# Sample attention one step deeper, new probabilities through the gate's bank, mask and decays stored once

## The chip, the cores and the metric

The kernel runs on one core of a Trainium2 chip. The metric is the device time of one execution in microseconds (us). The core has TensorE (PE, with its weight loads as PEld), VectorE (DVE), ScalarE (ACT), GpSimd (POOL), whose part here is to issue DMAs, and SyncE (SP), which issues the other DMAs. The accumulators lie in PSUM, 8 banks of 128 partitions by 512 float32.

## What is computed

It is one inference step of a two-layer encoder for 256 prompt rows and for 8 requests of 16 new rows ("samples") with 512 cached keys each. All is float32. A layer is a SwiGLU block, a token mixer and a second SwiGLU block. The mixer has three attention branches of 6 heads by 64:

```
sb:  a = sigmoid(z) * prod of sigmoid(-z) over the later keys (strictly causal)
fox: p = softmax(z + decay of the key's row and head)
dsa: p = softmax(z + mask), mask = the top 132 of 528 keys by an indexer's score
y = sum over the branches of sigmoid(gate_n) * (o_n @ w_branch_n);  out = y @ w_out
```

The change touches the samples' attention: 8 requests x 3 branches x 3 head pairs.

## The kernel before

One head pair of one request is a group. A unit is 4 groups, so that 4 groups x 2 heads x 16 queries fill 128 partitions. There are NU = 6 units for each branch and NSTEP = 18 steps in each layer, steps 0 to 5 for sb, 6 to 11 for fox and 12 to 17 for dsa. For unit s the work is:

- keys: `turn_three(s)` and `turn_fourth(s)` (L1113) transpose the cached keys of the 4 groups on PE, three into banks 0 to 2, the fourth into bank 3 or 0. ACT copies them to `KT[s % 2]` (L1611, L1612, L1617, `kt_free`).
- scores (L1187): 4 groups, banks 4 and 5. DVE adds the bias (L2328) and the mask of the new keys (L2333). For fox and dsa the bias comes from `BX[s % 2]`, loaded by POOL (L1718) from a DRAM scratch, and DVE takes the row maximum (L2341).
- ACT makes the probabilities: two sigmoids for sb (L1629, L1630) or Exp (L1632). For sb DVE then runs a reverse product scan (L2047) and a product (L2346).
- `turn_probs` (L1158) transposes the 512 old columns into bank 6, `turn_new_probs` (L1164) the 16 new ones into bank 7. DVE copies both to `PTS` (L2296, L2298).
- `values` (L1178) multiplies by the values into bank 7, `output_rows` on DVE (L2304 or L2306 and L2307) scales them into `OU`, `output` on PE (L1147) folds the rows into bank 7, and DVE copies them to `OT` (L2290).

PE's order in step s, written by hand, is: scores(s), output(s-2), turn_probs(s-1), turn_three(s+2), turn_new_probs(s-1), half a gate tile, values(s-1), turn_fourth(s+2). A gate half (L1138) is four of the eight k-slices of a tile of 384 columns in bank 3. Its sum stays open in that bank from one half to the next, and the twelve halves lie in the steps of `GATE_UNIT`. DVE's order is: scores' bias(s), output(s-2), copies of the probabilities(s-1), maximum or scan(s), rounds of the top-k, output_rows(s-1). One round (L2313, L2316) takes the 8 largest scores out of the indexer's rows. There are 17 rounds, in the steps of `ROUND_S`.

When the rounds are over, in step 9, SP stores the mask (L587): 8 DMAs write each row six times, once per head. The decays of fox are stored earlier (L539) with each row sixteen times. POOL's load for step 12 waits for the mask's store (`msk_stored`). Three buffers hold cached keys: the load of key block n (L572, SP's queue) waits until block n-3 has been transposed. Four buffers hold values (L1700, L1706, POOL's queue), and a load waits for `values` of the block four before. A block of keys or of values (one request, one branch) is 768 KB, and a step uses 4/3 of a block of either kind.

Of the kernel before, what the change touches and what calls it, by code (L numbers as in the profile page):

```python
# [20 lines left out]
P = 128  # L21
# [99 lines left out]
def unit_spans(s):  # L121

    out, i = [], 0
    while i < UNIT:
        n, a = unit_groups(s)[i]
        k = min(NPAIR - a, UNIT - i)
        out.append((i, i + k, n % NB, a))
        i += k
    return out

# [7 lines left out]
def program(nc, t):  # L138
    with ExitStack() as ctx:
# [121 lines left out]
        OU = NORM[:, (PC + 1) * P:(PC + 2) * P]  # L261
# [67 lines left out]
        ps_ready = sem("sprobs_ready")  # L329
        st_ready, st_copied = sem("st_ready"), sem("st_copied")  # L330
# [38 lines left out]
        def _(sp):  # L369
# [126 lines left out]
            for l in range(DEPTH):  # L496
# [5 lines left out]
                for i in range(N_PROJ):  # L502
# [75 lines left out]
                for s in range(-2, NSTEP):  # L578
# [5 lines left out]
                    if s == max(ROUND_S):  # L584
                        sp.wait_ge(msk_ready, l * 3 + 3)
                        for b in range(NB):
                            sp.dma_start(m_s[b * NH * NT:(b + 1) * NH * NT, :].rearrange("(h t) k -> t h k", t=NT),  # L587
                                         WKS[b * NT:(b + 1) * NT, :][:, None, :].to_broadcast([NT, NH, KEYS])).then_inc(msk_stored, 16)

                w = t["w_branch"][l].rearrange("n (k p) d -> p (n k) d", p=P)  # L590
                for i in range(N_BRANCH):
                    r = R_BRANCH + i
                    if i < 2:
                        sp.wait_ge(gate_ready, l * 24 + 21 + 3 * i)
                        sp.wait_ge(msk_stored, (l + 1) * NB * 16)
# [16 lines left out]
        def _(pe):  # L612
# [253 lines left out]
            for l in range(DEPTH):  # L866
# [248 lines left out]

                def turn_three(s):
# [6 lines left out]
                def turn_fourth(s):  # L1123

                    if s >= 2:
                        pe.wait_ge(kt_free, 3 * (l * NSTEP + s) + 2)
                    turn_group(s, 3, 3 if s < 2 else 0).then_inc(kt_ready, 1)

                def gate_half(n, half):

                    r = R_GATE + n // 3 - 1
                    if half == 0:
                        if n % 3 == 0:
                            full(l, r)
# [1298 lines left out]
```

## Time and profile before

| | |
|---|---|
| time, 3 runs | 2439.22 us median (2438.75 to 2440.55) |
| profiled execution | 2444.67 us, span 2442.9 us |
| busy over the span | PE 2366.5 (97%), PEld 2044.6, DVE 1240.9, ACT 555.7, POOL 75.3 us |
| DMA | 396.57 MB, mean 162 GB/s |
| mean granted TensorE clock | 0.992 |

The times of the table's first line are device times. The span is what the profiler recorded from the first instruction to the last, and the profiled execution took 1.8 us more than it. PE's busy share counts its pipelined matmuls, so 97% is not PE at its peak. Each layer has one sample attention, of 141 us, and both show the same pattern.

### The profile page before, as it was taken

Reading aid. Unit: us, or ns where it says so; the run is one execution under the profiler, and the core shown is the slowest. Engines: PE = TensorE matmul, PEld = TensorE weight load, DVE = VectorE, ACT = ScalarE, POOL = GpSimd, SP = SyncE. Lnnn points to the kernel's source line nnn. Section 1 sums busy time; section 2 is a strip of 40 time slices with the busy share of each in tenths; the row PEclk is TensorE's granted clock in tenths of the full one; section 3 lists DMA queues with packets and bytes.
Section 4 is the critical chain, followed back from the end, with each engine's and each line's share of the span. In section 5 each row is a group of like instructions: output and inputs, shape, how many; then the busy total and the mean of one; then the engine's idle time right before and its main releaser. Section 6 shows DMA issues by size and latency. Waiting matters only on the chain.

```text
span 2442.9 us, 41219 instructions
## 1 busy us (share of the span) xinstructions
PE 2366.5 (97%) x17088; PEld 2044.6 (84%) x17088; DVE 1240.9 (51%) x2630; ACT 555.7 (23%) x1290; POOL 75.3 (3%) x124
## 2 busy tenths in 40 slices
PE   7999999999998999999999999999999989999998
PEld 6999996886665589999989999878756656999998
DVE  3656422534665426565265663235365844366742
ACT  3000022113553322001130000211235432410011
POOL 0000000000022000000000000000000220000000
PEclk9999999999999999999999999999999999999999
DMA  8354243773389342542325533447634883323232
GB/s 322 128 186 162 95 143 122 234 251 100 117 282 338 130 152 103 181 164 93 133 104 177 185 135 108 146 145 255 203 104 169 306 295 126 105 83 125 95 117 74
DMA packets 298634, 396.57 MB, mean 162 GB/s; under 512 B 31309, under 2 KB 243145, under 8 KB 298450
## 3 DMA queue, kind: packets, MB, share of 16 engines
q1 hardware_dynamic: 278690, 339.66, 41.3%
q0 software_dynamic: 12672, 45.42, 5.3%
q10 hardware_dynamic: 7088, 8.87, 1.0%
q8 instruction: 136, 2.23, 0.4%
q14 instruction: 48, 0.39, 0.0%
HBM read 378.54 MB, written 15.37 MB: 161 GB/s over the span
## 4 chain that ended last, share of the span: by engine, by line
PE 88%; DMA 4%; DVE 3%; SPq 2%; ACT 2%; issue 1%; DVEq 0%; ACTq 0%; POOLq 0%
PE PS L681 30%; PE PS L779 12%; PE PS L986 6%; PE PS L1228 4%; PE PS L934 4%; PE PS L880 3%; PE PS L651 2%; PE PS L827 2%; PE PS L835 2%; PE PS L956 2%; PE PS L720 2%; PE PS L1113 2%; DMA BIG<-w_ada 2%; PE PS L1138 2%; PE PS L1250 2%; PE PS L1242 2%
## 5 line engine op out<-in xcount | busy, mean ns | idle before, releaser
L681 PE MATMUL PS<-OT,RING 128*128 128x192 f32 x1280 | 234.2, 326 | 0.0
L681 PE MATMUL PS<-H,RING 128*128 128x192 f32 x1280 | 223.4, 328 | 0.0
L681 PE MATMUL PS<-OT,QR 128*128 128x192 f32 x1280 | 221.1, 326 | 0.0
L681 PEld LDWEIGHTS PS<-OT,RING 128*128 128x128 f32 x1280 | 212.4, 190 | 0.0
L681 PEld LDWEIGHTS PS<-H,RING 128*128 128x128 f32 x1280 | 208.4, 190 | 4.4 <-issue 4.1
L681 PEld LDWEIGHTS PS<-OT,QR 128*128 128x128 f32 x1280 | 210.2, 190 | 0.0
L1356 ACT ACTIVATE QR<-QR 128x384 f32<-128x384 f32 x80 | 41.8, 522 | 530.9 <-DVE QR L1916 530.9
L986 PE MATMUL PS<-H,RING 128*128 128x384 f32 x480 | 160.9, 490 | 0.0
L986 PEld LDWEIGHTS PS<-H,RING 128*128 128x128 f32 x480 | 89.1, 190 | 61.5 <-issue 4.7
L681 PE MATMUL PS<-H,QR 128*128 128x192 f32 x640 | 117.1, 326 | 0.0
L681 PEld LDWEIGHTS PS<-H,QR 128*128 128x128 f32 x640 | 106.2, 190 | 0.0
L1916 DVE TENSOR_TENSOR QR<-PS,QR 128x384 f32<-128x384 f32 x80 | 44.6, 557 | 110.7 <-PE PS L681 110.7
L1228 PE MATMUL PS<-OT,RING 128*128 128x384 f32 x288 | 93.4, 487 | 0.8 <-DVE OT L2290 0.8
L880 PE MATMUL PS<-RING,H 128*128 128x384 f32 (+1 forms) x288 | 90.9, 472 | 0.0
L779 PE MATMUL PS<-BIG,RING 128*128 128x192 f32 x528 | 89.7, 326 | 0.0
L1228 PEld LDWEIGHTS PS<-OT,RING 128*128 128x128 f32 x288 | 54.6, 190 | 38.7 <-DVE OT L2290 1.0
L779 PEld LDWEIGHTS PS<-BIG,RING 128*128 128x128 f32 x528 | 86.5, 190 | 0.0
L1968 DVE TENSOR_TENSOR QR<-RING 128x768 f32<-128x768 f32 (+1 forms) x24 | 21.3, 889 | 125.8 <-DMA RING<-ffn_w_out 125.8
L1911 DVE TENSOR_TENSOR QR<-PS,QR 128x384 f32<-128x384 f32 x80 | 44.4, 555 | 79.6 <-PE PS L681 79.4
L1113 PE MATMUL PS<-IDENT,QKT 128*128 128x128 f32 x576 | 77.7, 279 | 6.8 <-DMA QKT<-cache_dsa_k 4.2
L880 PEld LDWEIGHTS PS<-RING,H 128*128 128x128 f32 x288 | 54.0, 190 | 32.3 <-issue 1.4
L1113 PEld LDWEIGHTS PS<-IDENT,QKT 128*128 128x128 f32 x576 | 63.7, 142 | 17.0 <-issue 6.7
(308 smaller groups left out, 4043.7 us busy)
## 6 DMA issues: line engine op xcount, KB each, us to landing
RING<-ffn_w_in SPq DMA_DIRECT2D x80, 1024.0 KB, 7.2
RING<-w_in SPq DMA_DIRECT2D x64, 768.0 KB, 6.1
QR<-w_ada SPq DMA_DIRECT2D x34, 1024.0 KB, 9.7
BIG<-w_ada SPq DMA_DIRECT2D x34, 1024.0 KB, 10.3
RING<-ffn_w_out SPq DMA_DIRECT2D x32, 768.0 KB, 4.6
RING<-ffn_w_out SPq DMA_DIRECT2D x32, 640.0 KB, 5.3
QR<-cache_sb_v POOLq DMA_DIRECT2D x16, 768.0 KB, 5.9
QKT<-cache_sb_k SPq DMA_DIRECT2D x16, 768.0 KB, 6.4
```

What stands on the lines that cost most here:

```text
L651: mm = pe.matmul(PS[32 * j:32 * j + 32, bank, col:col + P], CT[:, k, :], w[:, k, j * P:(j + 1) * P], start=(k == 0), stop=(k == KD - 1))
L681: mm = pe.matmul(PS[:, bank, GROUP[g]], a[:, k, :], x[:, k, :], start=(k == 0), stop=(k == 3))
L720: mm = pe.matmul(PS[:, PLAIN_BANK[p] + part, GROUP[1]], w[:, k, part * 256 + jj * P:part * 256 + (jj + 1) * P], H[:, k, GROUP[1]], start=( ...
L779: mm = pe.matmul(PS[:, bank, 0:HALF], a[:, k, :], x[:, k, :], start=(half == 0 and k == 0), stop=(half == 1 and k == kn - 1))
L827: mm = pe.matmul(PS[:, m, 0:HALF], w[:, k, m * P:(m + 1) * P], HID[:, half * k2 + k, GROUP[0]], start=(half == 0 and k == 0), stop=(half = ...
L835: mm = pe.matmul(PS[:, m + 2, 0:HALF], w[:, k, m * P:(m + 1) * P], HID[:, half * k2 + k, GROUP[1]], start=(half == 0 and k == 0), stop=(ha ...
L880: mm = pe.matmul(PS[:, n % 3, 0:width], H[:, k, tt * P:(tt + 1) * P], w[:, k, :], start=(k == 0), stop=(k == KD - 1))
L934: mm = pe.matmul(PS[:, bank, GROUP[half]], a[:, k, :], x[:, k, :], start=(k == 0), stop=(k == 3))
L956: mm = pe.matmul(PS[:, 4, 0:MIX], H[:, k, 2 * P:T], w[:, k, :], start=(k == 0), stop=(k == KD - 1))
L986: mm = pe.matmul(PS[:, bank, 0:T], w[:, k, (n % 3) * P:(n % 3 + 1) * P], H[:, k, :], start=(k == 0), stop=(k == KD - 1))
L1113: mm = pe.transpose(PS[:, bank, c * P:(c + 1) * P], KC[:, n % KBUF, c, a * P:(a + 1) * P], IDENT[:, :])
L1228: mm = pe.matmul(PS[:, n, 0:T], w[:, 3 * n + k, m * P:(m + 1) * P], OT[:, 3 * n + k, :], start=(k == 0), stop=(k == NPAIR - 1))
```

## The change

- One step deeper: PE does values(s-2) and output(s-3) in step s, right after the scores, and there are NSTEP + 2 steps. DVE and ACT follow it. `OU` has two buffers, the statistics in `ST` four columns in place of two.
- `scores(s)` waits for `sz_taken(s-1)`, the bias operation alone, in place of `zs_ready`.
- The 16 new columns of the probabilities are transposed into columns 384 to 511 of bank 3, and ACT copies them (`sn_copied`). For sb ACT copies the 512 old ones too (`PROBS_ACT`).
- A gate piece is all eight k-slices of one half of the columns (192), complete in its step and copied at once by ACT (`take_part`). `turn_fourth` always uses bank 3 and follows `turn_three` directly.
- On DVE the maximum follows the bias at once; the rounds of the top-k and the gate pieces lie in other steps.
- Mask and decays are stored once (one DMA each), and the loads of POOL repeat the rows: one DMA for the decays, two for the mask.

```diff
-GATE_UNIT = {u: (18 + i // 2, i % 2) for i, u in enumerate((0, 1, 2, 4, 5, 7, 9, 11, 13, 15, 17, 18))}
+GATE_UNIT = {u: (18 + i // 2, i % 2) for i, u in enumerate((0, 1, 3, 4, 6, 7, 9, 10, 12, 13, 15, 16))}
-ROUND_S = {0: 1, 1: 2, 2: 2, 3: 1, 4: 2, 5: 2, 6: 1, 7: 2, 8: 2, 9: 2}
+ROUND_S = {0: 2, 1: 2, 3: 2, 4: 2, 5: 1, 6: 3, 7: 3, 9: 2}
...
-OU = NORM[:, (PC + 1) * P:(PC + 2) * P]
+OU = [NORM[:, (PC + 1) * P:(PC + 2) * P], AR[:, :]]
...
-g_s = nc.dram_tensor("scr_g_sample", (NB * NH * NT, KEYS), F32, kind="Internal").ap()
+g_s = nc.dram_tensor("scr_g_sample", (NB * NH, KEYS), F32, kind="Internal").ap()
...
-m_s = nc.dram_tensor("scr_mask_sample", (NB * NH * NT, KEYS), F32, kind="Internal").ap()
+m_s = nc.dram_tensor("scr_mask_sample", (NB * NT, KEYS), F32, kind="Internal").ap()
...
-                sp.dma_start(g_s.rearrange("(g t) k -> g t k", t=NT),
-                             GX[0:48, :][:, None, :].to_broadcast([48, NT, KEYS])).then_inc(gs_stored, 16)
+                sp.dma_start(g_s, GX[0:48, :]).then_inc(gs_stored, 16)
...
-                for b in range(NB):
-                    sp.dma_start(m_s[b * NH * NT:(b + 1) * NH * NT, :].rearrange("(h t) k -> t h k", t=NT),
-                                 WKS[b * NT:(b + 1) * NT, :][:, None, :].to_broadcast([NT, NH, KEYS])).then_inc(msk_stored, 16)
+                sp.dma_start(m_s, WKS).then_inc(msk_stored, 16)
...
+        def part_copied(s):
+            if last_part(s):
+                n, half = last_part(s)
+                if half:
+                    pe.wait_ge(gate_taken, l * 24 + n + 1)
+                else:
+                    pe.wait_ge(half_taken, l * GATE_HALVES + n - GATE_FIRST_UNIT)
+        def turn_fourth(s):
+            part_copied(s - 1)
+            if s >= 3:
+                pe.wait_ge(sn_copied, l * NSTEP + s - 2)
+            turn_group(s, 3, 3).then_inc(kt_ready, 1)
...
+        def gate_part(s):
+            n, half = GATE_UNIT[s]
             r = R_GATE + n // 3 - 1
+            if half == 0 and n % 3 == 0:
+                full(l, r)
+            part_copied(s)
+            pe.wait_ge(kt_free, 3 * (l * NSTEP + min(s + 2, NSTEP)) + 1)
             w = ring(l, r, KD, MIX)
+            for k in range(KD):
+                mm = pe.matmul(PS[:, 3, 0:HALF], w[:, k, (n % 3) * P:(n % 3 + 1) * P], H[:, k, GROUP[half]],
                                start=(k == 0), stop=(k == KD - 1))
+            mm.then_inc(gate_ready if half else half_ready, 1)
+        def scores(s):
+            pe.wait_ge(kt_free, 3 * (l * NSTEP + s) + 4)
+            if l or s:
+                pe.wait_ge(sz_taken, l * NSTEP + s)
...
+            mm.then_inc(ss_ready, 1)
+        def values(s):
+            for n in sorted({n for n, _ in unit_groups(s)}):
+                pe.wait_ge(v_full[n % VBUF], l * (NCACHE // VBUF * 32) + 32 * (n // VBUF + 1))
+            pe.wait_ge(ou_ready, l * NSTEP + s + 1)
+            if l or s:
+                pe.wait_ge(o_free, l * NSTEP + s)
+            pe.wait_ge(st_copied, l * NSTEP + s + 1)
+            pe.wait_ge(sn_copied, l * NSTEP + s + 1)
...
+            mm.then_inc(pv_ready, 1)
...
         def turn_new_probs(s):
-            pe.wait_ge(o_free, l * NSTEP + s + 1)
-            pe.transpose(PS[0:NT, 7, 2 * P:3 * P], ES[s % 2][:, PAST:KEYS], IDENT[:, :]).then_inc(st_ready, 1)
+            pe.wait_ge(kt_free, 3 * (l * NSTEP + min(s + 3, NSTEP)) + 1)
+            if last_part(s + 1):
+                part_copied(s + 1)
+            if s:
+                pe.wait_ge(sn_copied, l * NSTEP + s)
+            pe.transpose(PS[0:NT, 3, 3 * P:4 * P], ES[s % 2][:, PAST:KEYS], IDENT[:, :]).then_inc(st_ready, 1)
         def step(s):
+            if s < NSTEP:
+                scores(s)
+            if 2 <= s:
+                values(s - 2)
+            if s >= 3:
+                output(s - 3)
+            if 1 <= s <= NSTEP:
                 turn_probs(s - 1)
+                turn_new_probs(s - 1)
+            if s in GATE_UNIT:
+                gate_part(s)
             if s + 2 < NSTEP:
                 turn_three(s + 2)
                 turn_fourth(s + 2)
...
+        def take_part(s):
+            n, half = GATE_UNIT[s]
+            if half:
+                act.wait_ge(gate_ready, l * 24 + n + 1)
+            else:
+                act.wait_ge(half_ready, l * GATE_HALVES + n - GATE_FIRST_UNIT)
+            A(G[:, n, GROUP[half]], PS[:, 3, 0:HALF], ACT.Copy).then_inc(gate_taken if half else half_taken, 1)
         def step(s):
             e = ES[s % 2]
+            p = s % 4
+            if s < NSTEP:
+                begin()
+                act.wait_ge(zs_ready, l * NSTEP + s + 3)
+                if s < NU:
+                    link(A(LS, ZS, ACT.Sigmoid, scale=-1.0))
+                    A(e, ZS, ACT.Sigmoid).then_inc(es_ready, 1)
+                else:
+                    A(e, ZS, ACT.Exp, bias=ST[:, p:p + 1], accum_out=ST[:, 8 + p:9 + p]).then_inc(es_ready, 1)
+            if PROBS_ACT and 1 <= s <= NU:
+                act.wait_ge(st_ready, 2 * (l * NSTEP + s - 1) + 1)
+                if s >= 2:
+                    act.wait_ge(pv_ready, l * NSTEP + s + 1)
+                A(PTS[:, 0:PC, :], PS[:, 6, :].rearrange("p (c q) -> p c q", q=P), ACT.Copy).then_inc(st_copied, 1)
+            if s in GATE_UNIT:
+                take_part(s)
+            if 1 <= s <= NSTEP:
+                act.wait_ge(st_ready, 2 * (l * NSTEP + s - 1) + 2)
+                if s >= 2:
+                    act.wait_ge(pv_ready, l * NSTEP + s + 1)
+                A(PTS[0:NT, PC, :], PS[0:NT, 3, 3 * P:4 * P], ACT.Copy).then_inc(sn_copied, 1)
+            if s + 2 < NSTEP:
                 turned_three(s + 2)
+                turned_fourth(s + 2)
...
-            rows = (g_s, m_s)[s // NU - FOX]
-            pool.dma_start(BX[s % 2], rows[s % NU * P:(s % NU + 1) * P, :]).then_inc(bx_full[s % 2], 16)
+            if s < 2 * NU:
+                g = s % NU * 2 * UNIT
+                pool.dma_start(BX[s % 2], g_s[g:g + 2 * UNIT, :][:, None, :].to_broadcast([2 * UNIT, NT, KEYS])).then_inc(bx_full[s % 2], 32)
+            else:
+                for i, j, b, a in unit_spans(s):
+                    pool.dma_start(BX[s % 2][2 * NT * i:2 * NT * j, :],
+                                   m_s[b * NT:(b + 1) * NT, :][None, :, :].to_broadcast([2 * (j - i), NT, KEYS])).then_inc(bx_full[s % 2], 16)
...
         def turned_probs(s):
-            dve.wait_ge(st_ready, 2 * (l * NSTEP + s) + 1)
-            V.tensor_copy(PTS[:, 0:PC, :], PS[:, 6, :].rearrange("p (c q) -> p c q", q=P))
-            dve.wait_ge(st_ready, 2 * (l * NSTEP + s) + 2)
-            V.tensor_copy(PTS[0:NT, PC, :], PS[0:NT, 7, 2 * P:3 * P]).then_inc(st_copied, 1)
+            if not (PROBS_ACT and s < NU):
+                dve.wait_ge(st_ready, 2 * (l * NSTEP + s) + 1)
+                V.tensor_copy(PTS[:, 0:PC, :], PS[:, 6, :].rearrange("p (c q) -> p c q", q=P)).then_inc(st_copied, 1)
...
             begin()
+            if s < NSTEP:
+                dve.wait_ge(ss_ready, l * NSTEP + s + 1)
+                if r != SB:
+                    dve.wait_ge(bx_full[s % 2], l * (NU * 32) + ((s - NU) // 2 + 1) * 32)
+                bias = (ZERO[:, :] if r == SB else BX[s % 2]).rearrange("p (s k) -> p s k", s=2)
+                link(V.scalar_tensor_tensor(out=ZS.rearrange("p (s k) -> p s k", s=2), in0=PS[:, 4:6, 0:264],
+                                            scalar=SCALE, in1=bias, op0=ALU.mult, op1=ALU.add))
+                dve.sem_inc(sz_taken, 1)
+                if r != SB:
+                    dve.sem_inc(bx_free, 1)
+                if r != DSA:
+                    link(V.tensor_tensor(ZS[:, PAST:KEYS], ZS[:, PAST:KEYS], (MSB, MFOX)[r][:, :], ALU.add))
+                if r != SB:
+                    link(V.tensor_reduce(ST[:, p:p + 1], ZS, AXX, ALU.max, negate=True))
                 dve.sem_inc(zs_ready, 1)
+            if s >= 3:
+                output(s - 3)
             if s >= 2:
+                output_rows(s - 2)
+            if 1 <= s <= NSTEP:
                 turned_probs(s - 1)
+            if s < NU:
                 dve.wait_ge(es_ready, l * NSTEP + s + 1)
```

## Rows read from the trace of the kernel before

**Rows 1.** Windows of the first layer's sample attention: busy us of each engine, granted clock, DMA share, GB/s.
```profile
727.00:770.00 43.00, 40.15 (x512) 27.68 (x505) 29.99 (x78) 19.91 (x34) 10.80 (x18) 1.00 0.94 322
...
742.00:747.00 5.00, 4.54 (x75) 3.14 (x73) 4.32 (x12) 2.91 (x5) 1.42 (x3) 1.00 1.04 381
...
777.00:782.00 5.00, 4.51 (x53) 2.82 (x56) 1.71 (x5) 1.43 (x3) 1.67 (x3) 0.50 0.95 357
```

**Rows 2.** Waits of PE, 672 to 823 us: us in total, times, longest.
```profile
PE PS L1164 <- DVE OT L2290: 3.8, 3, 2.9
PE PS L1178 <- DVE NORM L2298: 3.4, 7, 0.6
...
PE PS L1113 <- DMA QKT<-cache_dsa_k: 2.6, 2, 1.8
```

**Rows 3.** Timeline of PE, first layer: start us, us, line, tiles, count.
```profile
681.62 1.10 PE L1187 MATMUL PS<-QR,QBLK 128*32 128x264 f32 x16
...
760.93 1.10 PE L1187 MATMUL PS<-QR,QBLK 128*32 128x264 f32 x16
761.96 0.43 PE L1147 MATMUL PS<-OWN,NORM 128*128 128x64 f32 x2
762.23 0.61 PE L1158 MATMUL PS<-IDENT,QR 128*128 128x128 f32 x4
762.67 1.47 PE L1113 MATMUL PS<-IDENT,QKT 128*128 128x128 f32 x12
...
764.09 2.75 PE L1138 MATMUL PS<-H,RING 128*128 128x384 f32 x8
766.77 1.43 PE L1178 MATMUL PS<-QR,NORM 128*32 128x128 f32 x40
768.13 0.66 PE L1113 MATMUL PS<-IDENT,QKT 128*128 128x128 f32 x4
768.72 1.10 PE L1187 MATMUL PS<-QR,QBLK 128*32 128x264 f32 x16
...
822.58 2.85 PE L1228 MATMUL PS<-OT,RING 128*128 128x384 f32 x8 [0.38 <-DVE OT L2290]
```

**Rows 4.** Timeline of all engines, first layer, around the mask of the third branch.
```profile
755.78 4.69 SPq L587 DMA_DIRECT2D scr_mask_sample<-RING  x8
...
770.31 0.56 POOL L1718 DMA_DIRECT2D MASKS<-scr_mask_sample  x1 [12.42 <-DMA scr_mask_sample<-RING]
...
775.66 0.71 DVE L2328 SCALAR_TENSOR_TENSOR DMB<-PS,MASKS 128x528 f32<-128x528 f32 x1 [6.84 <-DMA MASKS<-scr_mask_sample]
...
777.73 2.28 PE L1178 MATMUL PS<-QR,NORM 128*32 128x128 f32 x33 [0.49 <-DVE NORM L2298]
```

**Rows 5.** Timeline of DVE, first layer: two scores of the first branch in a row.
```profile
711.61 0.71 DVE L2328 SCALAR_TENSOR_TENSOR DMB<-PS,ZERO 128x528 f32<-128x528 f32 x1
...
719.74 0.71 DVE L2328 SCALAR_TENSOR_TENSOR DMB<-PS,ZERO 128x528 f32<-128x528 f32 x1
```

**Rows 6.** Groups by line and shape, both layers: busy us, mean ns, idle before.
```profile
L2296 DVE COPY NORM<-PS 128x512 f32<-128x512 f32 x36 | 24.5, 681 | 0.6 <-PE PS L1158 0.3
...
L2298 DVE COPY NORM<-PS 16x128 f32<-16x128 f32 x36 | 9.9, 276 | 11.1 <-PE PS L1164 11.1
...
L1617 ACT ACTIVATE QR<-PS 128x512 f32<-128x512 f32 x36 | 21.5, 596 | 45.4 <-PE PS L1113 45.4
...
L1629 ACT ACTIVATE MASKS<-DMB 128x528 f32<-128x528 f32 x12 | 7.7, 645 | 17.6 <-DVEq L2335 17.6
```

**Rows 7.** DMA: landing of the key loads (L572), then issues by tile, us to landing.
```profile
DMA to landing us min/median/max: 4.3/6.4/12.3
...
QKT<-cache_dsa_k SPq DMA_DIRECT2D x16, 768.0 KB, 9.2
...
scr_mask_sample<-RING SPq DMA_DIRECT2D x16, 198.0 KB, 8.4
MASKS<-scr_mask_sample POOLq DMA_DIRECT2D x12, 264.0 KB, 6.1
```

More of the change, by code:

```diff
@@ L129, in unit_spans, with last_part @@
     return out
+def last_part(s):
+    before = [u for u in GATE_UNIT if u < s]
+    return GATE_UNIT[max(before)] if before else None
 def last_unit(n):
@@ new lines, in scores @@
+                def scores(s):
+                    pe.wait_ge(kt_free, 3 * (l * NSTEP + s) + 4)
+                    if l or s:
+                        pe.wait_ge(sz_taken, l * NSTEP + s)
+                    for half in range(2):
+                        for i, (n, a) in enumerate(unit_groups(s)):
+                            mm = pe.matmul(PS[32 * i:32 * i + 32, 4 + half, 0:264], QBLK[:, n // NB, a, n % NB, :],
+                                           KT[s % 2][:, i, half * 264:(half + 1) * 264], start=True, stop=True)
+                    mm.then_inc(ss_ready, 1)
@@ new lines, in values @@
+                def values(s):
[6 more added lines that the diff above has]
+                    pe.wait_ge(sn_copied, l * NSTEP + s + 1)
+                    for c in range(PC + 1):
+                        k = P if c < PC else NT
+                        for i, (n, a) in enumerate(unit_groups(s)):
+                            v = VC[n % VBUF][:, c, a * P:(a + 1) * P] if c < PC else VN[n % VBUF][0:NT, a * P:(a + 1) * P]
+                            mm = pe.matmul(PS[32 * i:32 * i + 32, 7, 0:P], PTS[0:k, c, i * 32:(i + 1) * 32], v,
+                                           start=(c == 0), stop=(c == PC))
+                    mm.then_inc(pv_ready, 1)
@@ L1210, in _ @@
                 pe.wait_ge(gate_taken, l * 24 + GATE_FIRST_UNIT + 1)
-                for s in range(NSTEP):
+                for s in range(NSTEP + 2):
                     step(s)
-                output(NSTEP - 2)
-                turn_probs(NSTEP - 1)
-                turn_new_probs(NSTEP - 1)
-                gate_half(*GATE_UNIT[NSTEP])
-                values(NSTEP - 1)
                 output(NSTEP - 1)
@@ L1642, in _ @@
                 turned_three(1)
-                for s in range(NSTEP):
+                turned_fourth(1)
+                for s in range(NSTEP + 2):
                     step(s)
-                take_gate(GATE_UNIT[NSTEP][0], 3)
                 act.wait_ge(gate_taken, l * 24 + 24)
@@ L2320, in step @@
                     e = ES[s % 2]
[L2321 removed]
+                    p = s % 4
                     begin()
[L2324 to L2329 removed]
@@ L2350, in step @@
                         V.tensor_scalar(WKS, WKS, TAKEN / 2, NEG, ALU.is_gt, ALU.mult).then_inc(msk_ready, 1)
-                    if s >= 1:
-                        output_rows(s - 1)
-                    if r == SB:
+                    if s < NU:
                         dve.wait_ge(ps_ready, l * NU + s + 1)
-                    else:
+                    elif s < NSTEP:
                         dve.wait_ge(es_ready, l * NSTEP + s + 1)
-                begin()
-                for s in range(NSTEP):
+                for s in range(NSTEP + 2):
                     step(s)
                 begin()
-                output(NSTEP - 2)
-                turned_probs(NSTEP - 1)
-                output_rows(NSTEP - 1)
                 output(NSTEP - 1)
```

101 lines of the change are left out of this document (14 added, 87 removed).

## The prediction

> **What bounds the kernel now.** I read the page first, for the busy shares, then the windows of the stage that the change touches, then PE's waits there, then the timelines of PE and DVE step by step, and last the DMA landings. PE is busy nearly everywhere, so a gain can only be PE's idle time in the two sample attentions, or work that goes away.
>
> A step with a gate piece is PE's work without a gap. It runs from 760.93 to 768.72, 7.79 us [rows 3]. Its parts, from start to start, are scores 1.03, output 0.27, old probabilities 0.44, three groups of keys and the new probabilities 1.42, the gate half 2.68, values 1.36, the fourth group 0.59. Without a gate piece that is 5.11. A layer needs 18 scores, outputs, values and pairs of turned probabilities (18 x 3.20 = 57.6 with 0.10 for the new ones), 16 x 1.91 = 30.6 for the keys and 12 x 2.68 = 32.2 for the gate, together 120.4. The stage takes from 681.62 to 822.58, 140.96 us [rows 3]. So 20.6 us in each layer are waits or slow clock.
>
> The waits have names. In steps without a gate piece PE reaches `values` too early and waits for DVE's copies of the probabilities (3.4 us), and it waits for DVE's copy of the outputs before the new probabilities (3.8) and for late keys (2.6) [rows 2]. DVE sets the pace while it has top-k rounds: two biases of sb lie 8.13 us apart, with two rounds between them, more than PE's 7.79 [rows 5]. The longest hole is step 12. The mask's eight stores start at 755.78, POOL can issue its load only at 770.31, after 12.42 us of waiting, and DVE stands until 775.66 (6.84 us) [rows 4]. PE then comes back at half speed: the granted clock is 0.50 in 777 to 782 [rows 1], the lower of its two levels, and the values' 33 matmuls take 2.28 us, where a step's 40 take 1.43 at full speed [rows 3, 4]. Layer two repeats this.
>
> DMA is the second limit. Its share is 0.94 with 322 GB/s in 727 to 770, and at saturation (1.04) it moves 381 GB/s [rows 1].
>
> **The change part by part.** Removed and moved on DVE: the copy of 0.68 us in the six sb units and that of 0.28 us in all 18 [rows 6]. ACT makes them. Its copy of 128x512 takes 0.60 [rows 6], and ACT is busy 19.9 of 43.0 us in the middle of the stage [rows 1], so their cost on ACT is hidden unless it delays a consumer (below). DVE's sb step of 8.13 loses 0.96. It now has only the output's copy and `output_rows` (0.6) to put beside ACT's two sigmoids of 0.65 each [rows 6], so it keeps 7.2 to 8.1 us. I take 7.55, just under PE's 7.79. DVE stops being the pace of gate steps. The rounds stay 17, and the steps with three of them are gate steps.
>
> The gate's matmuls: half as wide and twice as many, 16 of 192 columns for 8 of 384. PE streams the same columns. I take 2.68 again. If each of the 96 extra matmuls of a layer cost a tenth of the present 0.33 us, it would be 3 us a layer, so the bounds are 0 and 3. Twelve copies of ACT replace six, hidden.
>
> The deeper order: `values` follows the copies it needs by most of a step, so its waits [rows 2] go. In their place comes a chain through bank 3. `turn_fourth(s+2)` needs ACT's copy of the new probabilities(s-1), and ACT comes to it only after DVE's bias(s) (0.95 with the small mask), two sigmoids (1.35), the old probabilities (0.60), the gate piece (0.3) and itself (0.25), 3.5 us after DVE begins. Where DVE is behind PE, at the start, PE stands there. Queued behind it are scores(s+1), and nothing else of PE can pass. Step by step I get 6.5, 7.1 and 7.1 us for steps 0 to 2, that is 20.7. Then nine gate steps at 7.79 are 70.1, four without a gate piece at 5.11 are 20.4, and step 16, without keys, 5.9. The end (step 17 and the two drain steps) has three values, four outputs, two pairs of probabilities and one scores, 7.2 us of work, and its dependencies through DVE leave 3.5 us of holes, so 10.7. Sum 127.8, against 140.96: 13.2 us saved in a layer, if no DMA is late.
>
> The mask: one store of 264 KB in place of eight of 198 KB. By the steps above the rounds end some 4 us earlier, at about 751.5. With 0.3 for SP, a landing of 8.4, two POOL issues of the load (0.56 each [rows 4]) and a landing of 6.1 [rows 7] the bias arrives near 767.4. By my steps DVE wants it at 765.5. So about 2 us of the 6.84 stay, between 0 and 5 (8.4 and 6.1 together 2 us less or 3 more). I take it that the stall is then too short to bring the half clock back; if it did, the cost would be some 2 us more. The decays' store lies in the projection, where nothing in the traces waits for it: worth nothing in time.
>
> POOL's loads write as many bytes into SBUF as before. Rows repeated by the source cost no more that I can see, and there are about 11 us between issue and use in all but steps 7 and 12. I take nothing, with bounds of 0 and 2 us a layer. The Trainium skill ("DMA: Bandwidth & Descriptors", the section on why a DMA increments its semaphore by 16) says that a DMA runs on the largest number of engines up to 16 that divides the outermost dimension of both sides. By it the decays' load (8 by 16 rows) would use 8 engines and the mask's loads 2 to 6, each with 16 rows in place of 8. As an estimate, an engine that moves 381/16 = 24 GB/s needs 1.4 us for 34 KB in place of 0.7 us, so the sum would be 1.4 us a layer longer if both critical loads showed it. No row of before shows such a load.
>
> **The keys' window** is what I subtract. `turn_fourth` now follows `turn_three` at once. Key block 4j+1 is asked for when `turn_three` of unit 3j-1 is done and is needed by `turn_fourth` of unit 3j. That was a full step and what stood between the two, gate and values (9.3 to 11.9 us by the starts in [rows 3]). It is one gate step now, 7.73, or 7.5 after the issue. Key loads land in 6.4 us at the median, dsa's in 9.2, the slowest in 12.3 [rows 7]. The stage also asks for more: five steps from 7 to 11 in 33.5 us need 10.5 MB of keys and values and 1.8 of masks and the rest, 367 GB/s, near the 381 of a saturated stretch [rows 1]. So the landings should be like dsa's: 1.7 us for each of the three blocks 13, 17 and 21, 5.1 us a layer. Bounds are 0 (6.4) and 14.4 (12.3 at each). The mask's 2 us fall into the delay of block 17, two steps before, and aren't added.
>
> 13.2 - 5.1 = 8.1 us a layer, 16.2 in both. The profiled execution's 2444.67 would become 2428.5 (its span 2426.7); it lay 5.4 above the median, and the median 2439.22 becomes **2423**.
>
> **Rivals.**
> - A: PE-bound, DMA keeps up. The landings stay near 6.4, since the mask's 1.3 MB less leave the queue. 13.2 x 2 gives 2413. For: the stage moves 322 GB/s and can move 381 [rows 1]. Against: the share is 0.94 already.
> - B: ACT or DVE becomes the pace. The chain through bank 3 shows in more than the first steps, because ACT's queue is strict and each late bias delays the key copies of two steps on. If each of the six steps 3 to 8 lost 1 us, the gain is 13.2 - 5.1 - 6 = 2.1 a layer: 2435. For: DVE's 7.55 is only 0.24 under PE's step, and steps 6 and 7 have three rounds. Against: ACT has no long operation in fox.
> - C, slower: the keys' window. It holds for all five blocks 4j+1 (5, 9, 13, 17, 21). The gain of 13.2 is eaten when each waits 2.6 us, so when they land later than 10.1 us after the issue. At the slowest 12.3 it is 5 x 4.8 = 24 a layer: 2461. For: dsa's median is 9.2. Against: the stage's median is 6.4.
> - D: the shortened mask path doesn't help: the store queues behind blocks 17 and 18 and the load is as late as now. Then 5 us a layer of the gain go, 2433.
>
> **How the numbers follow.** Chances: forecast 0.52, A 0.15, B 0.12, C 0.08, D 0.13. The range is 2411 to 2436. It holds A, B, D and the extra gate cost (3 us a layer), and leaves out C and what lies beyond A. 0.2% is 4.9 us, about what a measurement can tell from no change, so faster means under 2434.3: forecast and A wholly, D and B mostly, 0.85. Within it fall the slow part of B and D and a little of C, 0.09. Slower is C, 0.06.
>
> **What the changed profile would show.** PE's waits for DVE's copies (L2298) gone from `values`. A step without a gate piece at 5.1 to 5.3 us. `turn_fourth` waiting for ACT in steps 0 to 2, and for dsa keys in steps 10 and 13. DVE's wait at step 12 under 3 us and the granted clock at 1.00 through the stage. The stage 130 to 135 us long in each layer, the rest of the kernel unchanged. I would be wrong if gate steps take over 8 us throughout (rival B or dearer gate matmuls), if step 12 still shows a clock of 0.50 (D), or if the keys' landings pass 10 us (C).

## The result, and the profile after

| kernel | median us (lowest to highest) | ratio to before, 95% interval | profiled span us |
|---|---|---|---|
| before | 2439.46 (2437.44 to 2442.53), 20 runs | | 2442.9 |
| after | 2446.53 (2439.97 to 2453.16), 20 runs | 1.0026 [1.0019, 1.0033] | 2442.6 |

I had predicted 2423 us (2411 to 2436). The change made the kernel 7 us slower, by 0.26%, which the interval separates from no change. Its runs also scatter more: 13 us where before has 5.

The stage, from the first scores to the first matmul of the branch, should have shrunk from 140.96 us [rows 3] to 132.9. It takes 141.64 us in layer one (677.75 to 819.39) and 141.88 in layer two, where before took 139.97. So nothing of the predicted gain is left in the stage, and the question is where it went. The 7 us above before are a smaller matter. Against a second profile of before (experiment 8) the kernel after is 4.5 us longer, of which 2.3 are in the two stages and 1.9 behind the second one.

PE's timeline of the kernel after, layer one: the end of step 2, its hole and the scores behind it, steps 6 to 8, and the first matmuls behind the stage in layer two.

```profile
694.20 1.47 PE L1119 MATMUL PS<-IDENT,QKT 128*128 128x128 f32 x12
698.28 1.09 PE L1119 MATMUL PS<-IDENT,QKT 128*128 128x128 f32 x4 [2.61 <-issue]
699.30 1.99 PE L1166 MATMUL PS<-QR,QBLK 128*32 128x264 f32 x16
...
720.50 1.10 PE L1166 MATMUL PS<-QR,QBLK 128*32 128x264 f32 x16
...
723.58 2.77 PE L1155 MATMUL PS<-H,RING 128*128 128x192 f32 x16
726.19 1.91 PE L1119 MATMUL PS<-IDENT,QKT 128*128 128x128 f32 x16
728.03 1.10 PE L1166 MATMUL PS<-QR,QBLK 128*32 128x264 f32 x16
...
736.63 0.63 PE L1119 MATMUL PS<-IDENT,QKT 128*128 128x128 f32 x4 [1.45 <-DMA QKT<-cache_fox_k]
737.19 1.10 PE L1166 MATMUL PS<-QR,QBLK 128*32 128x264 f32 x16
...
745.22 1.62 PE L1119 MATMUL PS<-IDENT,QKT 128*128 128x128 f32 x8 [3.92 <-DMA QKT<-cache_fox_k]
746.77 1.99 PE L1166 MATMUL PS<-QR,QBLK 128*32 128x264 f32 x16
...
2021.05 11.31 PE L1249 MATMUL PS<-OT,RING 128*128 128x384 f32 x29 [0.38 <-DVE OT L2333]
```

Read it from scores to scores. The gate step 720.50 to 728.03 is 7.53 us without a hole. The next, 728.03 to 737.19, has a hole of 1.45 us for a key block. The one from 737.19 to 746.77 has no gate piece and should take 4.92; it takes 9.58, since PE waits 3.92 us for keys and then transposes and scores at half speed (1.99 us for the 16 matmuls of the scores in place of 1.10).

PE's waits in the stage of layer one, kernel after (line of PE, then what ended the wait; us in total, times, longest):

```profile
PE PS L1119 <- DMA QKT<-cache_fox_k: 5.4, 2, 3.9
PE PS L1119 <- DMA QKT<-cache_dsa_k: 3.5, 2, 2.9
PE PS L1119 <- issue: 2.6, 1, 2.6
PE PS L1184 <- DVE NORM L2340: 2.4, 2, 1.3
PE PS L1119 <- ACT BIG L1647: 1.7, 2, 1.1
```

The waits of [rows 2] for DVE's copies are down from 7.2 to 2.4 us, as predicted. The waits for keys went from 2.6 to 8.9 us (in layer two from 1.6 to 4.0).

Windows of the kernel after (busy us of PE, PEld, DVE, ACT, POOL, then granted clock, DMA share, GB/s), against [rows 1]. The last but one lies in step 12 of layer two, the last one follows that layer's stage:

```profile
691.34:706.00 14.66, 12.05 (x158) 9.28 (x158) 10.05 (x20) 6.95 (x13) 2.60 (x4) 0.88 0.58 177
...
724.00:729.00 5.00, 5.00 (x51) 4.44 (x53) 4.68 (x12) 3.09 (x6) 1.39 (x3) 1.00 1.08 283
729.00:734.00 5.00, 5.00 (x70) 4.56 (x63) 3.86 (x11) 1.70 (x6) 3.01 (x5) 1.00 1.03 244
744.00:749.00 5.00, 3.78 (x36) 2.43 (x40) 0.18 (x1) 2.08 (x3) 0.00 (x0) 0.66 1.02 291
...
724.00:767.00 43.00, 37.63 (x468) 31.51 (x467) 27.20 (x70) 18.17 (x38) 13.21 (x22) 0.96 1.01 305
...
1979.00:1984.00 5.00, 5.00 (x60) 2.99 (x60) 1.84 (x3) 2.03 (x4) 0.00 (x0) 0.50 1.04 315
...
2021.05:2031.05 10.00, 10.00 (x26) 5.77 (x27) 2.79 (x5) 6.84 (x7) 0.00 (x0) 0.83 0.01 2
```

The DMA share is over 1 and yet only 244 to 291 GB/s move, where before moved 381 at such a share. The engines' records are full, but not with bytes. Over 43 us the share rose from 0.94 to 1.01 and the rate fell from 322 to 305.

DMA issues of the kernel after, both layers (KB each, median us from issue to landing), then the landings of all key loads (its L580):

```profile
QKT<-cache_fox_k SPq DMA_DIRECT2D x16, 768.0 KB, 9.0
...
MASKS<-scr_g_sample POOLq DMA_DIRECT2D x12, 264.0 KB, 8.9
...
scr_mask_sample<-RING SPq DMA_DIRECT2D x2, 264.0 KB, 9.8
...
DMA to landing us min/median/max: 4.3/7.8/17.2
```

Against [rows 7] and the same views of before: the key loads' median rose from 6.4 to 7.8 us, the slowest from 12.3 to 17.2, fox's from 5.2 to 9.0, and the decays' loads, which now repeat their rows, from 4.9 to 8.9.

### The profile page after: what moved, and what is told of

Same layout as the page of the kernel before. It is cut to its first block, busy times and chain, and to the rows that moved or that the text cites. A ratio compares the mean times of both kernels' runs of the same rounds, so it can differ in the third digit from the quotient of the medians.

```text
span 2442.6 us, 41762 instructions
## 1 busy us (share of the span) xinstructions
PE 2363.5 (97%) x17280; PEld 2078.6 (85%) x17280; DVE 1224.1 (50%) x2582; ACT 567.1 (23%) x1350; POOL 85.3 (3%) x136
## 2 busy tenths in 40 slices
DMA packets 298957, 390.87 MB, mean 160 GB/s; under 512 B 34350, under 2 KB 246186, under 8 KB 298771
## 4 chain that ended last, share of the span: by engine, by line
PE 87%; DMA 5%; DVE 2%; ACT 2%; SPq 1%; issue 1%; DVEq 0%; POOL 0%; ACTq 0%; POOLq 0%
PE PS L687 30%; PE PS L785 12%; PE PS L992 6%; PE PS L940 4%; PE PS L1249 4%; PE PS L886 3%; PE PS L657 2%; PE PS L833 2%; PE PS L962 2%; PE PS L841 2%; PE PS L726 2%; DMA BIG<-w_ada 2%; PE PS L1271 2%; PE PS L1263 2%; PE PS L1119 2%; PE PS L1155 1%
```

## The experiments

Medians of before on the same chips were 2440.5, 2440.0, 2440.3, 2439.9 and 2440.5 us in the five sessions. The lengths of steps and stages below are differences of PE's starts in the timeline, as above. Each comes from one profiled execution, which need not lie at the median: those of `decays_in_16_groups` (2435.25 us), `loads_of_16_rows` (2437.41), `plain_loads` (2437.76) and `best_decays_16_row_loads` (2438.22) are the fastest of their kernels.

**1. Take the repeated loads away, or only add them.** `plain_loads` is the kernel after with these lines as they were in before; `once_only` is before with them as in after. Of the decays the diff shows store and load, without their semaphores; the mask's store and loads change in the same way:

```diff
-sp.dma_start(g_s, GX[0:48, :])
+sp.dma_start(g_s.rearrange("(g t) k -> g t k", t=NT), GX[0:48, :][:, None, :].to_broadcast([48, NT, KEYS]))
...
-pool.dma_start(BX[s % 2], g_s[g:g + 2 * UNIT, :][:, None, :].to_broadcast([2 * UNIT, NT, KEYS]))
+pool.dma_start(BX[s % 2], rows[s % NU * P:(s % NU + 1) * P, :])
```

> The changed kernel, but mask and decays are stored with every row repeated and loaded by one plain DMA of 128 rows, as in the kernel before. Theory L (the loads that repeat their source rows take DMA capacity from the key and value loads): the key loads land in 5 to 9 us again, PE waits for keys under 3 us a layer, and the time is 2420 to 2430, 10 to 18 us under the kernel before. Theory W (the new order asks too late for key block 4j+1, whatever the form of the loads): key waits stay at 5 to 10 us a layer and the time is 2438 to 2448.

> The kernel before, with only the storage of mask and decays changed: stored once, rows repeated by the loads. Theory L: slower than before by 3 to 15 us (2442 to 2454), bias loads landing in 8 to 12 us in place of 5 and key loads over 10 us. Theory W: faster than before by 5 to 12 us, since the decays' store gives 2 to 3 us in a layer and the mask's stores about 3.

`plain_loads` took 2440.04 us, 0.9998 [0.9989, 1.0007]; `once_only` 2446.09, 1.0025 [1.0012, 1.0039]. The whole loss is in the loads and stores of bias rows, with either order of PE's work. In `plain_loads` PE waits 0.3 us or less for keys in a stage, so there the shorter window for block 4j+1 costs nothing. Its gate steps 6, 7, 9, 10 and 15 all take 7.5 us. Much of what it gains it gives back in step 12, 13.65 and 14.14 us long, where DVE waits 10.0 and 10.5 us for the eight stores of the mask and its load. Its stages (136.33 and 139.07 us) are still 5.9 us shorter together than those of before's second profile. Only 2.1 of them reach the span: 1.3 are lost ahead of the first stage and 2.2 behind the second, where the granted clock is 0.81 in the first 10 us.

**2. Which property of a repeated load?** `loads_of_16_rows` cuts each load in eight DMAs of 16 partitions; `rows_in_halves` cuts the rows in two pieces of 264 columns; `three_dims_distinct` stores the rows repeated and loads distinct rows in the shape 8 x 16.

> The changed kernel, but each load of mask or decays is cut into eight DMAs of 16 partitions, each with 16 rows outermost on both sides; the rows are still stored once and repeated by the source. Theory L in the form of few engines for each DMA (8 or 2 to 6, by the outermost dimension): these loads spread over 16 engines, land in 4 to 6 us, and the time is 2417 to 2428. Theory L in the form that repeated source rows are slow in themselves: no better than the changed kernel, 2440 to 2450. Theory W: 2440 to 2450, with short landings of the bias loads.

> The changed kernel, but each repeated load is issued for 264 columns at a time, so a row of 528 goes as two pieces of 1056 bytes. Theory S (in the repeated loads each row of 2112 bytes is cut into 2048 and 64 bytes, and the 64-byte packets are dear): packets under 512 bytes fall back by some 1500 in the stage, key loads land as in plain_loads, and the time is 2432 to 2438. Theory K (a load on 8 or fewer engines is what costs): the engines stay the same, the time is 2443 to 2452, as for the changed kernel.

> The changed kernel with the repeated stores of before, and loads of distinct rows, but in the shape of the repeated loads (8 or 2 to 6 groups outermost, by 16 rows). Theories S and K: as slow as the changed kernel or slower by the larger stores, 2443 to 2452, and it shows the same extra small packets. Theory R (reading the same row again is what costs): as plain_loads, 2438 to 2442.

Measured 2442.71 us, 1.0014 [1.0003, 1.0026]; 2440.65, 1.0000 [0.9991, 1.0010]; 2440.73, 1.0005 [0.9996, 1.0014]. The second lies between its two theories, and 5.9 us under the kernel after, though it repeats the same rows. Theory S is out all the same: packets under 512 bytes rose from 34350 to 34925 in the execution, while PE's waits for keys fell from 8.9 and 4.0 us to 2.3 and 2.4. What the two pieces change is told in experiment 5. I read the last as "the shape costs nothing", too soon: its rows lie one behind the other, so the shape 8 x 16 may not have reached the hardware. Experiment 5 shows that it had not. Of the cut loads experiment 7 tells more.

**3. The mask's stall.** `rounds_end_at_8` is `plain_loads` with `8: 2` in place of `9: 2` in ROUND_S; `rounds_8_expand_late` also stores the decays once and repeats them from DRAM to DRAM later; `rounds_8_keys_first` is the first with the mask's stores put behind the key load of step 9 in SyncE's queue; `decays_expanded_late` is `plain_loads` with the late repetition alone.

> plain_loads with the last two rounds of the top-k in step 8 in place of step 9. Theory M (the mask's eight stores and its load take about 20 us after the last round, whatever PE does, so each us that the deeper order gains before step 12 is waited out there): step 12 shortens from about 14 to 8 to 10 us in each layer, step 8 grows by 1 to 2, and the time is 2430 to 2435. Theory W (the keys' window): no change, 2438 to 2442.

> rounds_end_at_8, and the decays are stored once, then repeated from DRAM to DRAM while the queues are quiet, before the prompt attention. The store of 1.6 MB in the projection cost 2.5 us in the first layer and 0.5 in the second, so 2427 to 2432.

> rounds_end_at_8 (plain loads, the last choosing rounds in step 8), with the eight stores of the mask put behind the key load of step 9 in the SyncE queue. Theory Q (step 10 took 16 us there because the wait for the mask and the 8.5 us of issuing stood ahead of a key block in SyncE's queue): step 10 falls back to 7.5 to 10 us, step 12 stays near 7.5 to 10, the stage takes 130 to 134 us, and the time is 2434 to 2438 us. Rival W (the transfers themselves, 1.6 MB written while keys are read, hold up the keys, wherever they are issued): some step from 9 to 12 still takes 12 us or more, and the time is 2440 to 2445 us.

> plain_loads, with the decays stored once in the projection and repeated from DRAM to DRAM by one transfer behind the gate biases, ahead of the sample attention. Theory S (the store of 1584 KB in the projection costs 2.5 us in layer 1 and 0.5 in layer 2, and the same bytes are free at the later place): 2437 to 2438.5 us. Rival: the transfer is paid where it now lies, by the prompt attention's late loads: 2440 us or more.

Measured 2445.27 us, 1.0018 [1.0010, 1.0027]; 2443.57, 1.0015 [1.0006, 1.0023]; 2438.92, 0.9996 [0.9987, 1.0005]; 2441.27, 1.0002 [0.9993, 1.0011]. In the first, step 12 fell to 7.5 us and step 10 rose to 16. Neither theory had that. The reason is in SyncE's queue and in PE's longest wait:

```profile
746.62 8.49 SPq L596 DMA_DIRECT2D scr_mask_sample<-RING  x8
755.22 18.55 SPq L581 DMA_DIRECT2D QKT<-cache_dsa_k  x4
...
PE PS L1122 <- DMA QKT<-cache_dsa_k: 7.9, 1, 7.9
```

A key block was issued only at 755.22, behind 8.49 us of stores. With the keys first step 10 is 7.5 us again, as theory Q said, and 6.4 us come back. But step 12 is 13.70 and 12.83 again: theory Q's 2434 to 2438 missed, because the stores, now late, make the mask late. In neither of these two orders do the eight stores leave both steps short. The late repetition of the decays gains nothing beyond the interval (rival), and the 2427 to 2432 of `rounds_8_expand_late` missed by over 11 us. It also speaks against a reading of mine of the kernel after, whose stage begins at 677.75 us and not at 681.62, that the small store had won time in the projection. The second profile of the kernel before (experiment 8), with the large store, begins its stage at 677.51.

**4. Mask and decays apart.** Only one of the two is stored once and repeated:

> The kernel after, with only the mask stored once and repeated by its loads; the decays are stored repeated and loaded plainly, as before the change. Theory D (the six repeated loads of the decays, in the steps in which keys are loaded too, are what costs): the stall of plain_loads at step 12 (13.65 and 14.14 us) shrinks to 8 to 11 us as in the kernel after, no key block is late before step 10, and the time is 2435 to 2438 us. Theory M2 (the repeated loads of the mask cost as much as those of the decays): steps 9 and 13 grow, and the time is 2441 to 2445 us.

> The kernel after, with only the decays stored once and repeated by their loads; the mask is stored eight times and loaded plainly. Theory D: the key waits of the kernel after return in steps 3, 7 or 8 (DMA fox_k, dsa_k), step 12 keeps plain_loads' 13 to 14 us, and the time is 2444 to 2448 us, less at most the 2.5 us that the small store gave in the projection. Theory M2: like plain_loads, 2439 to 2441 us, since the mask's loads, now plain, were the cost.

| | decays plain | decays repeated |
|---|---|---|
| mask plain | 2440.04 (`plain_loads`) | 2445.61, 1.0021 [1.0012, 1.0030] |
| mask repeated | 2434.83, 0.9982 [0.9973, 0.9991] | 2446.53 (after) |

Theory D holds. The mask's part of the change gains 5.2 us beside plain decays and nothing beside repeated ones (2445.61 against 2446.53), and the decays' part costs 5.6 with the mask plain and 11.7 with it repeated. The mask's repeated loads cost too (they land in 7.5 to 9.1 us, before 6.1), but less than the seven stores that they save. PE waits 4.7 and 4.4 us for dsa's keys in its stages.

**5. Why the decays' loads cost.** The packets of POOL's queue can be counted in the trace by start and length. For the decays' loads (packets of 4224 bytes, 64 in a load), at a time is the median over a layer's six loads of the most that overlap:

```
kernel                  at a time, layers 1/2    mean us of a packet, layers 1/2
before (2nd profile)    16 / 15                  0.22 / 0.22
plain_loads             14.5 / 16                0.19 / 0.19
after                    9 / 9.5                 0.28 / 0.28
decays_repeated_only    10 / 9                   0.28 / 0.26
decays_in_16_groups     14 / 9.5                 0.25 / 0.25
best_decays_16_groups   12.5 / 12                0.26 / 0.24
rows_in_halves          14 / 13.5                0.26 / 0.28
three_dims_distinct     13 / 17.5                0.19 / 0.19
```

The count at a time is a sign of how many engines a load uses, and no more than that: when the queue is crowded a load across all of them shows few as well (the 9.5 above). A layer's first decays load is the clearest, with 10 at a time in both layers of the kernel after, 18 with 16 groups and 16 and 19 in `plain_loads`. So a repeated load of 8 rows by 16 seems to keep some 8 engines busy (the ends overlap a little), with packets half as long again: 64 x 0.28 = 18 us of engine time in place of 12, on half of the engines. As an estimate that is 2.2 us on each where a plain load puts 0.8. My reading is that a key block, spread over all engines, then lands when the busiest of them is done; the trace has no row for a single engine, so this step is argued and not shown. The Trainium skill ("DMA: Bandwidth & Descriptors", the section on why a DMA increments its semaphore by 16) says that the engines are the largest number up to 16 that divides the outermost dimension of both sides; by it this load has 8, and the trace agrees as far as 9 to 10 packets at a time go. `three_dims_distinct` has 13 and 17.5 at a time, so its rows did not go out as 8 x 16, and it was no test of the shape. A source with 16 rows outermost tests that: each row is stored twice, and a load reads 16 rows of 8 repeats.

```diff
-pool.dma_start(BX[s % 2], g_s[g:g + 2 * UNIT, :][:, None, :].to_broadcast([2 * UNIT, NT, KEYS]))
+pool.dma_start(BX[s % 2], g_s[2 * g:2 * g + 4 * UNIT, :][:, None, :].to_broadcast([4 * UNIT, NT // 2, KEYS]))
```

> The kernel after, but each row of the decays is stored twice, so that the repeated load has 16 source rows of 8 repeats outermost instead of 8 of 16. Same bytes into SBUF, same one transfer per unit, the source still repeated. The packets of the decays' loads of the kernel after never ran on more than 8 to 10 engines at a time and took 0.28 to 0.31 us each, against 12 to 19 engines and 0.17 to 0.25 us for plain loads. Theory E (a repeated load runs only on as many engines as there are rows outermost, so half of the 16 engines carry the whole load, and a key block lands with its slowest engine): now all 16 work, the key waits of steps 7 to 9 go, and the time is 2433 to 2437 us, that of mask_repeated_only. Theory R (reading a row of DRAM again and again is what costs): 2443 to 2447 us, as before.

2441.21 us, 1.0008 [0.9999, 1.0018], between the theories. So the wider load is worth 5.3 us of the decays' 11.7. The other 6.4 stay with repeated rows. `rows_in_halves` agrees: it issues each load as two DMAs of 8 groups, 13.5 to 14 packets are on their way at a time, and 5.9 us come back. It also settles another rival. Each repeated load of the kernel after has 64 further packets of 8 bytes, which those with 16 groups lack. In `rows_in_halves` there are as many, of 16 bytes, and the gain is there.

**6. The mask's loads in pieces of 16 rows.** `mask_repeated_only`, with each load of the mask cut in eight DMAs of 16 distinct rows; or with the rounds ending in step 8 and the keys first:

```diff
-for i, j, b, a in unit_spans(s):
-    pool.dma_start(BX[s % 2][2 * NT * i:2 * NT * j, :], m_s[b * NT:(b + 1) * NT, :][None, :, :].to_broadcast([2 * (j - i), NT, KEYS]))
+for x in range(2 * UNIT):
+    b = (s % NU * UNIT + x // 2) // NPAIR
+    pool.dma_start(BX[s % 2][NT * x:NT * x + NT, :], m_s[b * NT:(b + 1) * NT, :])
```

> mask_repeated_only, with the mask's loads cut in eight transfers of 16 distinct rows, so that each has 16 rows outermost. Theory E: the mask's loads land in 5.5 to 6.5 us instead of 7.5 to 9.8, steps 12 to 14 lose 2 to 3 us of their excess, and the time is 2431 to 2434 us. Rival: the eight issues of POOL for each load (0.6 us each) take back what the landing gains, and the time is 2434 to 2437 us.

> mask_repeated_only, with the last choosing rounds in step 8 and the mask's one store behind the key load of step 9. Theory: the bias of step 12 is there in time, steps 12 to 14 fall from 26.5 us to 21 to 23, and the time is 2428 to 2432 us. Rival: the wait of step 12 to 14 is the keys' (DMA dsa_k 4.7 us in three waits), not the mask's; it stays, and the time is 2433 to 2436 us.

The cut loads gave 2429.86 us, 0.9951 [0.9938, 0.9965], and once more, as the base of experiment 7, 2429.25, 0.9963 [0.9950, 0.9977] (five runs each). This beats both kernels, by 10 and 17 us. The loads land in 5.8 us. PE's waits for dsa's keys, 4.7 and 4.4 us in `mask_repeated_only`, are 0.4 and 0 in the second profile of this version; in the first they are 0 and 4.1. The earlier rounds gave 2436.24, 0.9982 [0.9973, 0.9991], nothing: the rival held, steps 12 to 14 wait for dsa's keys (3.4 and 5.0 us in a stage), not for the mask.

Two windows of the second run of this version, the one of above and the first 10 us behind the first stage:

```profile
724.00:767.00 43.00, 41.39 (x548) 35.37 (x547) 27.32 (x70) 20.02 (x41) 18.63 (x34) 1.00 0.99 341
...
810.80:820.80 10.00, 10.00 (x26) 5.83 (x27) 2.79 (x5) 5.56 (x6) 0.00 (x0) 0.83 0.00 0
```

PE is busy 41.39 of 43 us (after: 37.63), and 341 GB/s move at a share of 0.99 (after: 305 at 1.01).

**7. What of the decays is repetition and what the number of DMAs?** The best version with the decays' plain loads cut in eight as well, or with the 16 groups of experiment 5:

> mask_repeated_16_row_loads, with the decays' plain loads of 128 distinct rows cut in eight transfers of 16 distinct rows as well. loads_of_16_rows had such cut loads of a repeated row and took 2442.7 us, mask_repeated_16_row_loads 2429.9. Theory R (reading the repeated row costs, also with 16 rows outermost): 2429 to 2432 us. Theory I (POOL's eight issues per load, 48 a layer, and 128 small packets more per load, in the steps in which keys are short, cost): 2437 us or more.

> mask_repeated_16_row_loads, with the decays stored twice and their loads repeated as 16 rows of 8. Against decays_in_16_groups (2441.2) it has the mask's loads cut. If those were what kept it from theory E's 2433 to 2437: 2430 to 2433 us, and then the number of engines was the cost of the decays' loads. Theory R: at least 3 us above mask_repeated_16_row_loads of the same session.

> mask_repeated_16_row_loads again, on the same chip and beside the two others, for their comparison: 2428 to 2432 us, ratio 0.994 to 0.997.

Measured 2443.01 us, 1.0014 [1.0005, 1.0023]; 2437.62, 0.9988 [0.9977, 0.9998]; 2429.25. Cutting the decays' distinct rows into 48 DMAs a layer costs 13.8 us (theory I). For the mask the cut gained 5, but there it replaced repeated loads of 2 to 6 groups, and here plain loads of 128 rows, so the two don't compare the same thing. Repeating the rows costs 8.4 us even with 16 groups (theory R). Both have one row in common that the base doesn't show, the landing of the mask's store, first of the 16 groups, then of the cut loads, then of the base:

```profile
scr_mask_sample<-RING SPq DMA_DIRECT2D x2, 264.0 KB, 12.8
```
```profile
scr_mask_sample<-RING SPq DMA_DIRECT2D x2, 264.0 KB, 11.4
```
```profile
scr_mask_sample<-RING SPq DMA_DIRECT2D x2, 264.0 KB, 7.5
```

Their step 12 takes 11.0 to 11.4 us, that of the base 8.7 and 9.6. Why the store is late then wasn't settled: the decays' cut loads add 672 packets under 512 bytes to a stage's 2048, but the mask's repeated loads add 1120 to those of `plain_loads` and gain.

**8. The kernel before, profiled again.**

> The kernel before, unchanged, for a second profiled execution: the first lay 5.4 us above its own median. If the two sample attentions take 280 us in it again, the median's missing 5 us lie elsewhere; if they take about 276, the first execution's stages were longer than usual, and the sum of the prediction started from a stage that no median execution has.

2439.92 us, span 2438.1, stages 139.99 and 141.28. The stages are as long as in the first profile (140.96 and 139.97); the first execution's extra 5 us lay outside. So the sum started from the right stage, and the way from the profile to the median was right.

## Why the prediction was wrong, point by point

**The step that failed** is "POOL's loads write as many bytes into SBUF as before ... I take nothing, with bounds of 0 and 2 us a layer". For the decays it measured 11.7 us in both layers beside the repeated mask: 5.9 a layer, three times the upper bound. The mask's loads add 5.0, so the term comes to 16.7 of the 23.5 us by which the forecast missed. I had the rule of the Trainium skill (the same page and section) in the text, with 8 engines for this load, and priced it as the load's own lateness (0.7 us more for the decays' bytes on an engine), which has 11 us of cover. The price falls on the neighbour: fox's key blocks landed in 9.0 us at the median where before has 5.2 and `plain_loads` 6.1, and PE waited for them. That they wait for the engines with the bias rows is the likeliest reason, not a shown one. Nor did I count that such packets take 0.28 us for 0.19 to 0.22; why they do stays open.

**The keys' window.** I took 1.7 us for blocks 13, 17 and 21, 5.1 a layer. With plain loads the waits for keys were 0.3 us or less, so the mechanism costs nothing by itself (rival A's premise was right), though the stall of step 12 gives the last two blocks time there. The best version, without that stall, waits 0.4 us at most in one profile, and 4.1 in one layer of the other. With the repeated loads PE waited 8.9 us for keys in layer one, fox's first, and 4.0 in layer two. The two long waits of layer one (3.92 and 2.86 us) were followed by half speed, that of 1.45 us was not. This is rival C's form (blocks of all branches, landings beyond 10 us) with another cause than C's.

**The steps' own length** held. Steps 0 to 2 take 21.5 us (predicted 20.7), a gate step 7.52 (7.79), one without a gate piece 4.92 (5.11), step 16 5.77 (5.9), the end 11.5 (10.7). In the sum 126.2 for 127.8. The 16 narrow gate matmuls cost nothing extra (2.77 us a piece). Rival B is out: PE's waits for ACT and DVE in the stage sum to 6.2 us in layer one, most of them in the first steps and the end. In layer two they are 8.6, but 3.5 of these are ACT standing behind DVE's wait for the mask. The other 15.4 us of layer one are step 3 (0.9, half speed), 5 (0.3), 7 to 9 (7.4, keys and half speed), 12 to 14 (6.8, mask, keys and half speed). In layer two steps 7 and 8 have 6.1 and steps 12 and 13 have 8.0.

**The mask.** "About 2 of the 6.84 stay." DVE's timeline in the kernel after, step 12 of layer one and of layer two:

```profile
773.08 0.71 DVE L2371 SCALAR_TENSOR_TENSOR DMB<-PS,MASKS 128x528 f32<-128x528 f32 x1 [5.66 <-DMA MASKS<-scr_mask_sample]
...
1975.94 0.71 DVE L2371 SCALAR_TENSOR_TENSOR DMB<-PS,MASKS 128x528 f32<-128x528 f32 x1 [8.04 <-DMA MASKS<-scr_mask_sample]
```

In layer one another wait of 2.51 us followed in step 13: store and load, at 8.4 and 6.1 in the sum, took 7.7 and about 8.4. In layer two the store took 12.0 us and DVE waited 8.04, longer than the 6.6 of before. PE came back at a clock of 0.50 (1979 to 1984), and steps 12 and 13 took 11.70 and 11.34 us. That is rival D's own sign, in one layer of two. Put alone, the mask's part gained 5.2 us in both layers; with its loads cut in pieces of 16 rows 10.2 and 10.8. The idea was right and was mis-sized by its landings. The decays' store was indeed worth nothing.

**The clock.** I wrote "the granted clock at 1.00 through the stage". The hole of step 2 (2.61 us in the chain through bank 3, which I had foreseen as a stand but not as a clock) is followed by the level of 1.2 GHz: 0.88 in 691 to 706, while before held 1.00 there. Most stages of the new order lose so: their steps 2 and 3 take 16.4 to 16.7 us together. Those of `decays_in_16_groups`, with a clock of 1.00, take 15.0, and so do those of layer one alone in `loads_of_16_rows` and `best_decays_16_groups`. So this isn't a property of a version. A second place lies behind the stage. The end's holes leave 0.83 in the first 10 us, in layer two of the kernel after and in layer one of the best version (0.85 in its layer two), while before has 1.00 and so has layer one of the kernel after: some 1.6 us each time.

**What that leaves.** The best version's stages take 133.49 and 133.73 us in its second profile, the predicted 132.9 within a microsecond. That is luck: the terms differ (hardly a wait for keys where I took 5.1 us a layer, and an end of 13.8 us in place of 10.7), and the first profile of the same kernel has 132.56 and 136.55. It ends 6 us above 2423: 1.4 in the stages, 3.2 from half speed behind them, and the rest within the scatter. One chance was also placed wrongly: "D and B mostly" were counted as under 2434.3, where B's own time is 2435.

## What to carry to other kernels

A DMA's cost is not its own landing alone: ask on how many engines it runs and which transfer with a tight deadline shares them. Here the decays' loads, for which nobody waited, put over 5 us of waits for keys into a stage (`decays_repeated_only`: 5.8 and 5.4, `plain_loads`: 0.3 or less). Storing once and repeating in the load pays where it removes a store from a path that somebody waits for (the mask, 10 us when loaded in pieces of 16 rows), and costs where the store was free and the loads meet others (the decays, 6 us, and 12 beside the repeated mask). Parts of a change that look like one ("stored once, repeated by the loads") are worth a table of two by two before they are judged together.

## What was unexpected of the hardware

- A DMA share over 1 does not mean that the bytes are at their limit: 244 GB/s at 1.03 with repeated rows, 381 at 1.04 without. Packets of 4224 bytes took 0.28 us when their source rows were repeated, 0.19 to 0.22 when not.
- The same bytes in more DMAs can be dear: 48 cut loads of the decays a layer in place of six cost 13.8 us, with the same rows from the same places. Why wasn't tried.
- The same hole is not followed by the same clock. In step 2 PE waits 2.61 us in nearly every stage with the new order. In the kernel after the scores that follow take 1.99 us and the window around has a clock of 0.88; in `decays_in_16_groups` they take 1.10 us, and the window 691.5 to 706.1 has 1.00. In `loads_of_16_rows` both happen in one execution, 1.10 us in layer one and 1.99 in layer two. What decides between the two was not tried.
